# Two lines of SyncE's program exchanged at the end of the gates' stage: the last pair's diagonal blocks and the last gate tile's weights are fetched ahead of storing the third pair's inverses

## What is computed

```python
p = h @ w_in[l]
p_rwkv, p_mla, p_gate = jnp.split(p, [RWKV_COLS, RWKV_COLS + MLA_COLS], axis=-1)
y_rwkv = _rwkv7_mix(p_rwkv, ...)          # holds the scan below
...
gate_rwkv, gate_mla = jnp.split(jax.nn.sigmoid(p_gate), N_BRANCHES, axis=-1)

def step(S, inp):                          # one token of the scan
    r_t, w_t, k_t, v_t, kk_t, a_t = inp
    s_kk = jnp.einsum('bhvk,bhk->bhv', S, kk_t)
    S = (S * w_t[:, :, None, :] - s_kk[..., :, None] * (kk_t * a_t)[:, :, None, :]
         + v_t[..., :, None] * k_t[:, :, None, :])
```

## Time and profile before

| | us |
|---|---|
| median of 3 runs | 3614.34 |
| lowest and highest run | 3610.72, 3620.01 |
| profiled execution, its own time | 3616.57 |
| profiled execution, its span | 3614.8 |

### The profile page before, as it was taken

The page is one execution under the profiler, slowest core; times in us unless marked ns, Lnnn a source line. Parts: engine busy times, 40 slices in busy tenths (PEclk is TensorE's granted clock), DMA queues, the critical chain, the costliest instruction groups (busy, mean ns, idle before and its releaser), DMA issues. The chain is left out here.

```text
span 3614.8 us, 68870 instructions
## 1 busy us (share of the span) xinstructions
PE 3506.0 (97%) x29191; PEld 3288.5 (91%) x29191; DVE 2355.3 (65%) x2823; ACT 1317.3 (36%) x1900; POOL 1552.6 (43%) x877
## 2 busy tenths in 40 slices
PE   6999999999999999999999999999989999999998
PEld 6878999888998999999988799998879989999997
DVE  2474348665759877777835733585656697777777
ACT  5353035223114344453544520541231244444535
POOL 5475920001742665544445679000036346565441
PEclk9999999999999999999999999999999999999999
DMA  5522866423422222273235258463234122222732
GB/s 123 154 62 81 260 200 189 143 63 106 132 65 77 83 77 83 77 267 127 78 67 153 54 164 270 159 186 106 74 118 127 47 89 77 83 77 84 268 129 79
DMA packets 476186, 438.99 MB, mean 121 GB/s; under 512 B 106027, under 2 KB 401159, under 8 KB 475895
## 3 DMA queue, kind: packets, MB, share of 16 engines
q1 hardware_dynamic: 455640, 383.02, 35.1%
q10 hardware_dynamic: 20255, 51.78, 3.8%
HBM read 297.14 MB, written 137.05 MB: 120 GB/s over the span
## 5 line engine op out<-in xcount | busy, mean ns | idle before, releaser
L234 PE MATMUL psum<-h_hi,w_hi 128*128 128x348 f32 x1632 | 356.6, 327 | 9.7 <-ACT lat_sq L1235 3.7
L234 PE MATMUL psum<-h_lo,w_hi 128*128 128x348 f32 x1632 | 348.8, 322 | 0.0
L234 PE MATMUL psum<-h_hi,w_lo 128*128 128x348 f32 x1632 | 347.8, 321 | 0.0
L234 PEld LDWEIGHTS psum<-h_hi,w_hi 128*128 128x128 f32 x1632 | 274.6, 189 | 21.3 <-ACT lat_sq L1235 3.9
L234 PEld LDWEIGHTS psum<-h_lo,w_hi 128*128 128x128 f32 x1632 | 276.7, 188 | 0.0
L234 PEld LDWEIGHTS psum<-h_hi,w_lo 128*128 128x128 f32 x1632 | 275.4, 188 | 0.0
L3266 POOL TENSOR_TENSOR piece_lo_w<-sum,piece_hi_w 128x512 fp32r<-128x512 f32 x120 | 209.6, 1746 | 141.2 <-ACT piece_hi_w L3567 138.1
L3311 PE MATMUL psum<-t_hi,piece_hi_w 128*128 128x260 f32 x1280 | 258.2, 283 | 5.1 <-issue 2.6
L3311 PE MATMUL psum<-t_lo,piece_hi_w 128*128 128x260 f32 x1280 | 257.3, 282 | 0.0
L3311 PE MATMUL psum<-t_hi,piece_lo_w 128*128 128x260 f32 x1280 | 257.3, 282 | 0.0
L280 POOL TENSOR_TENSOR w_hi<-w_raw,consts 128x1024 fp32r<-128x1024 f32 (+1 forms) x80 | 134.0, 1675 | 284.1 <-PE psum L234 103.7
(11 more groups left out here) (653 smaller groups left out, 9709.1 us busy)
## 6 DMA issues: line engine op xcount, KB each, us to landing
w_raw<-in_w_in SPq DMA_DIRECT2D x68, 512.0 KB, 9.2
wsum<-in_w_down SPq DMA_DIRECT2D x88, 256.0 KB, 4.0
wsum_scratch<-wsum SPq DMA_DIRECT2D x22, 1024.0 KB
raw_g<-in_w_up SPq DMA_DIRECT2D x40, 512.0 KB, 3.8
raw_v<-in_w_up SPq DMA_DIRECT2D x40, 512.0 KB, 3.8
gate_scratch<-gst ACTq DMA_DIRECT2D x32, 522.0 KB, 3.0
gbuf<-gate_scratch SPq DMA_DIRECT2D x32, 522.0 KB, 3.7
prep_scratch<-prep ACTq DMA_DIRECT2D x8, 2080.0 KB, 8.0
```

What stands on the lines that cost most here:

```text
L234: last = nc.tensor.matmul(bank[:, n, :], w(k), x(k)[:, nrange(n)], start=(k == 0 and q == 0), stop=(k == kt - 1 and q == 2))
```

## The change

After the loop, SyncE's next three calls are put in another order: `blocks_in(3)` and `weights(15)` come ahead of `inverses(2)`. Nothing is added or removed; the same transfers are issued, with the same waits. It acts once in each of the two layers.

```diff
                 pairs_out(RT - 1)
-                inverses(RT - 2)
                 blocks_in(RT - 1)
                 weights(NGT - 1)
+                inverses(RT - 2)
                 sp.wait_ge(prep_out.sem, prep_out.of(RT))
```

## The result

The changed kernel takes 3620.79 us in the median of 12 runs (3616.62 to 3626.52), the kernel before 3615.38 in the median of 12 runs beside them (3609.68 to 3622.40). The ratio is 1.0018, with an interval of 1.0011 to 1.0026: slower by 6.5 us, 4.0 to 9.4; the two medians themselves lie 5.4 us apart. That is a loss of less than the 0.3% that was named as the bound, as forecast, and 3.8 us above the forecast time of 3617.

What follows compares the result with a forecast made beforehand. TensorE, busy 97%, was taken to bound the kernel. The solve's lateness less SyncE's wait at the barrier gave 1.15 + 1.4, +2.6 us in all; on the median of 3614.34 this made 3617 us, range 3608 to 3625.

Steps and rivals of the forecast that it cites:

- The order of arrival: At the barriers closing the stage TensorE comes last, so an earlier SyncE gains nothing; the stage ends with G15.
- The spare time: SyncE's wait for TensorE at the stage's barrier, 3.0 and 2.4 us, taken as room to hide lateness.
- The uncovered wait: On SyncE, blocks_in(3) waits for the pair's stores to land, no longer covered by eight store issues: 3.75 us.
- The first rival: Hidden altogether: pair's stores land in 1.4 us, the barrier opens as before, 3614.3 us; chance 0.20.
- The two fetches' issues: On SyncE, issuing blk and w_raw ahead of the inverse stores takes 0.85 us, the queue having drained.
- The eight stores' issues: On SyncE, issuing the third pair's inverse stores, behind both fetches, takes 6.40 us.
- Their landing: From the last inverse store's issue on SyncE to VectorE's clearing of ti: 2.4 us, the middle value.
- The lateness of the solve: The last solve on VectorE runs late by 4.15 us in the first layer and 3.8 in the second.
- lo15 stayed covered: On VectorE lo15 ends 5.4 and 5.1 us before G14 is taken out, enough to hide 4.15 and 3.8 us.
- The sum: Lateness beyond SyncE's wait at the barrier: 1.15 us and 1.4 us, +2.6 in all, +0.5 to +8.7.
- The clock: Rival: TensorE's low clock after the barrier goes away, up to 3.1 us per layer back, 3608 us; chance 0.12.
- The slow rival: SyncE held until clearing comes 17.7 and 17.4 us after the pair's stores; over 5.4 us lost per layer; chance 0.06.

Runs made afterwards that it cites:

- the kernel with half the cover given back: Changed kernel, but ti's four inverse stores go ahead of the two fetches and tit's four behind; ratio 1.0000 (0.9991 to 1.0008) against the kernel before.

## Why the prediction was right, and where its sum was off

The order of arrival. TensorE was last at the barrier before, and a SyncE that comes earlier gains nothing: shown by the kernel with its own ti, which comes 2.8 and 1.9 us earlier and measures the same.

The spare time was mis-sized. The prediction took all of SyncE's wait for TensorE as spare, 3.0 and 2.4 us. Of it 0.5 and 0.2 us are left in every profile in which SyncE comes last, so the true spare time was 2.5 and 2.2 us. The curve gives the same: in the second profile of the changed kernel the product is 3.45 us later than before and the stage 0.95 longer, so 2.5 were hidden; in the second layer 3.17 - 1.00 = 2.2.

The uncovered wait: 3.75 us was taken, 3.80 and 3.78 came (3.3 to 3.8 in the other profiles with this order). The first rival, a landing in 1.4 us and no loss, is thereby out. So is the estimate of some 2 us: the 2.0 us of the Trainium skill (DMA: Bandwidth & Descriptors, Anatomy of one DMA) are given there for transfers that GpSimd issues, and SyncE issues these.

The two fetches' issues: 0.85 was taken, 0.89 and 0.93 came. The value was right, the reason for it was not: in the first layer w_raw's issue of 0.42 us came behind the same unbroken run as the 1.58 in the second. The eight stores' issues: 6.40 against 6.17 and 6.66. Their landing: 2.4 against 2.04 and 2.05. Together, from the pair's stores to the clearing, 13.4 against 12.9 and 13.5.

What comes off: 0.38 us for blk in the first layer, as said. The lateness of the solve: 4.15 and 3.8 us were forecast, 3.64 and 3.85 came.

lo15 stayed covered, by 1.75 and 1.24 us after the change. The kernel with the stores behind the chunk loads shows what the cover was worth: there G15 came out 14.81 and 17.05 us after G14, where 11.45 is usual.

The sum: +2.6 us was forecast for the two stages; they lost 3.9, 2.0 and 2.1 us in the three profiles. The 3.9 holds one landing of 2.5 us that was 1.5 in the other two. The smaller spare time and the somewhat shorter lateness offset each other. That the sum comes near the stages' loss is in part luck: in the first layer both sizes were too large by 0.5 to 0.7 us.

The time moved by more than the stages: by 6.5 us (4.0 to 9.4), 5.1 (1.8 to 8.0) and 5.1 (1.8 to 8.3) in the three comparisons. The two later intervals hold the stages' 2 us, the first reaches down to 4.0, about the 3.9 of its own profile. The rest, 2.6 to 3.1 us by the ratios, is not explained. It is no more than these comparisons leave open: the kernel before against itself has an interval of -2.2 to 4.3 us. The stretches outside the two stages scatter by more than that from one profile to the next of the same program (3530.3 to 3537.4 us), so no place in them can be named, and whether there is a second, smaller loss stays open.

The clock. The stretch at the lower level stayed and moved with the stage's start: after the change, in the busy time by stretch that answers to the earlier trace rows (columns as there),

```profile
714.00:717.00 3.00, 2.23 (x9) 1.47 (x8) 2.77 (x6) 0.00 (x0) 0.00 (x0) 0.60 0.42 50
717.00:720.00 3.00, 2.77 (x11) 2.10 (x12) 1.70 (x5) 0.00 (x0) 0.00 (x0) 0.50 0.40 49
720.00:725.00 5.00, 4.82 (x29) 3.33 (x27) 3.02 (x5) 1.97 (x4) 0.00 (x0) 0.86 0.72 223
```

the granted clock is 0.60, 0.50 and 0.86, so the rival did not come. From the first load of the next stage to TensorE's first product with the inverses (L2053) it took 12.17 and 13.10 us before and 11.98 and 13.10 after. This stretch scatters: both layers together, it took 25.3 and 24.5 us in the two profiles before and 25.1, 24.1 and 25.3 in the three after, so nothing is lost or regained there by the change.

The rival's gain exists all the same. Of the twenty such stretches in the ten profiles one does not show the lower level at all, the second layer of the kernel with half the cover given back:

```profile
2492.00:2495.00 3.00, 1.95 (x13) 1.43 (x14) 2.26 (x6) 0.00 (x0) 0.00 (x0) 1.00 0.40 49
2495.00:2498.00 3.00, 3.00 (x24) 2.21 (x23) 2.32 (x5) 1.85 (x4) 0.00 (x0) 1.00 0.56 78
```

There the stretch took 10.24 us, and 11.68 to 13.87 in the other nineteen. Why the clock did not fall that once is not shown. The slow rival needed 17.7 us to the clearing; 12.9 and 13.5 came.

## What to carry to other kernels

In a queue that waits in order, a transfer's issue time can be another transfer's cover: the eight stores that were moved back had stood in front of a wait of 3.8 us at no cost, and behind it they paid for it. Before something is fetched earlier, look for who waits for it: the blocks were not what the solve waited for, the stores were, and the solve was not what the stage waited for. And of a wait at a barrier only the part above what the last engine to arrive still shows is spare.

## What the runs showed of the hardware

SyncE, when it is the last engine to arrive at this barrier, still shows a wait for TensorE of 0.5 us in the first layer and 0.2 in the second, the same in all the profiles in which it came last.

Four stores of the pair's blocks and four of tit carry the same bytes (52.8 KB a store), the first in runs of 104 bytes, the second of 2704. SyncE's wait after the last issue was 3.3 to 3.8 us for the pair's stores in the changed order, and 1.4 to 1.6 us (once 2.5) for the last stores of tit at the barrier. That the length of the runs is the cause is not shown.

In one profile, a load placed ahead of stores on the same queue cost the work behind them more than its issue: w_raw's issue takes 0.5 us, but with it alone in front the solve began 1.0 and 1.5 us later. In the first layer the clearing came 0.5 us later and blk's landing the other 0.5; in the second, beyond w_raw's issue, it was the stores' landing, 4.2 us after their last issue where it had been 3.2.

TensorE's clock after a pause: in the kernel with the stores behind the chunk loads, G15 began after a pause of 3.09 us in the first layer and 3.88 in the second. The busy time by stretch right after each (granted clock third from the end):

```profile
705.00:708.00 3.00, 3.00 (x19) 3.00 (x20) 2.72 (x9) 0.00 (x0) 0.00 (x0) 1.00 0.05 19
...
2490.00:2494.00 4.00, 4.00 (x20) 4.00 (x20) 3.59 (x13) 0.00 (x0) 0.00 (x0) 0.72 0.02 4
```

In the first layer it came back at the full level, in the second at the lower one (0.50 from 2488.90 to 2490.00), which reached into the stretch shown. The first group of three products took 0.75 us and 1.24 us, and G15 came out 17.05 us after G14 instead of 14.81: of the 2.24 us between them 0.8 is the longer wait for lo15.
